# Moving the adaLN row sums into the retention loop, in batches of four

## The reference

```python
def reference(x, c, ..., w_ada, b_ada, final_g):
    c_act = jax.nn.silu(c)
    for l in range(DEPTH):
        mod = c_act @ w_ada[l] + b_ada[l]                   # 1024 -> 6 * 1024, one row
        shift1, scale1, gate1, shift2, scale2, gate2 = jnp.split(mod, N_MOD, axis=-1)
        h = _modulate(_rmsnorm(x, norm_mix_g[l]), shift1, scale1)
        x = x + gate1[:, None, :] * _mixer(h, w_in[l], w_ret_out[l], w_sb_out[l], w_mix_out[l])
        h2 = _modulate(_rmsnorm(x, norm_mlp_g[l]), shift2, scale2)
        u = jnp.square(jax.nn.relu(h2 @ w_up[l]))
        x = x + gate2[:, None, :] * (u @ w_down[l])
    return _rmsnorm(x, final_g)
```

## Time and profile before

| | us |
|---|---|
| median of 3 runs | 2580.16 (2579.53 to 2580.59) |
| the profiled execution, first to last instruction | 2577.3 |
| PE busy | 2436.3 (95%) |
| DVE busy | 1147.3 (45%) |
| ACT busy | 890.2 (35%) |
| POOL busy | 901.7 (35%) |

### The profile page before, as it was taken

One profiled execution on the slowest core, in us unless ns is written; L12 is line 12 of the kernel. 1 busy time (PEld: TensorE's weight loads), 2 busy tenths in 40 slices (PEclk: granted clock), 3 DMA queues, 4 the chain that ended last, 5 costly groups with the idle time before them and its releaser, 6 DMA issues.

```text
span 2577.3 us, 32158 instructions
## 1 busy us (share of the span) xinstructions
PE 2436.3 (95%) x11946; PEld 1991.6 (77%) x11946; DVE 1147.3 (45%) x1535; ACT 890.2 (35%) x1005; POOL 901.7 (35%) x382
## 2 busy tenths in 40 slices
PE   6999999999998889999979999999999988999898
PEld 5887887888877667777867888888888866777786
DVE  6343243144446872552454323233444487552623
ACT  2222222255582232222322222224556613222232
POOL 1333433433332323433433343333332323433342
PEclk7999999999999999999999999999999998999999
DMA  6222222211125633433222232222112354433421
GB/s 216 92 86 82 96 77 82 95 63 59 62 67 174 200 99 102 144 128 98 98 79 79 73 103 66 90 94 67 64 65 66 98 178 145 145 121 113 130 93 55
DMA packets 252462, 260.62 MB, mean 101 GB/s; under 512 B 4145, under 2 KB 250049, under 8 KB 252353
## 3 DMA queue, kind: packets, MB, share of 16 engines
q1 hardware_dynamic: 250816, 255.92, 30.7%
q10 hardware_dynamic: 1536, 3.17, 0.4%
HBM read 256.97 MB, written 2.10 MB: 101 GB/s over the span
## 4 chain that ended last, share of the span: by engine, by line
PE 73%; DVE 15%; issue 4%; ACT 4%; DMA 3%; DVEq 0%; SPq 0%; ACTq 0%
PE proj L695 45%; PE proj L732 11%; DVE ada_sum L962 8%; PE proj L717 5%; PE att L830 3%; PE att L784 3%; DVE work L1222 3%; PE att L815 2%; PE att L842 1%; PE att L771 1%; DMA w_raw<-in_w_mix_out 1%; DMA work<-in_w_ada 1%; DVE ada_sum L960 1%; ACT w_hi L403 1%; ACT y_hi L606 1%
## 5 line engine op out<-in xcount | busy, mean ns | idle before, releaser
L365 POOL TENSOR_TENSOR w_lo<-w_raw,w_hi 128x1024 fp32r<-128x1024 f32 x368 | 899.5, 2448 | 1637.4 <-ACT w_hi L403 1637.1
L695 PE MATMUL proj<-h_hi,w_hi 128*128 128x512 f32 x1472 | 591.7, 402 | 10.5 <-DVE x_T L1035 9.4
L403 ACT ACTIVATE w_hi<-w_raw 128x1024 fp32r<-128x1024 f32 x368 | 385.3, 1054 | 612.0 <-PE proj L695 443.7
L695 PE MATMUL proj<-h_hi,w_lo 128*128 128x512 f32 x1472 | 578.0, 393 | 0.0
L695 PE MATMUL proj<-h_lo,w_hi 128*128 128x512 f32 x1472 | 577.5, 392 | 0.0
L695 PE MATMUL proj<-y_hi,w_hi 128*128 128x512 f32 x832 | 333.1, 400 | 21.2 <-DVE y_lo L1225 21.0
L695 PEld LDWEIGHTS proj<-h_hi,w_hi 128*128 128x128 f32 x1472 | 279.3, 190 | 72.8 <-issue 13.5
L695 PE MATMUL proj<-y_lo,w_hi 128*128 128x512 f32 x832 | 329.7, 396 | 0.0
L695 PE MATMUL proj<-y_hi,w_lo 128*128 128x512 f32 x832 | 329.5, 396 | 0.0
L695 PEld LDWEIGHTS proj<-h_hi,w_lo 128*128 128x128 f32 x1472 | 278.9, 189 | 59.9
L695 PEld LDWEIGHTS proj<-h_lo,w_hi 128*128 128x128 f32 x1472 | 279.4, 190 | 59.2 <-issue 3.8
(11 more groups left out here) (147 smaller groups left out, 2630.3 us busy)
## 6 DMA issues: line engine op xcount, KB each, us to landing
w_raw<-in_w_in SPq DMA_DIRECT2D x88, 1024.0 KB, 5.1
work<-in_w_ada SPq DMA_DIRECT2D x56, 1024.0 KB, 5.3
w_raw<-in_w_up SPq DMA_DIRECT2D x32, 1024.0 KB, 6.1
w_raw<-in_w_down SPq DMA_DIRECT2D x32, 1024.0 KB, 5.0
w_raw<-in_w_ret_out SPq DMA_DIRECT2D x16, 1024.0 KB, 4.9
w_raw<-in_w_sb_out SPq DMA_DIRECT2D x8, 1024.0 KB, 6.3
w_raw<-in_w_mix_out SPq DMA_DIRECT2D x8, 1024.0 KB, 7.8
ya<-in_x SPq DMA_DIRECT2D x1, 2048.0 KB, 8.3
```

The lines of the kernel that those rows point to most:

```text
L365: pool.tensor_tensor(w_lo[:, s, :, :], w_raw[:, s // 2, :, P * (s % 2):P * (s % 2 + 1)], w_hi[:, s, :, :], ALU.subtract).then_inc(lo_ready, 1)
L403: act.activation(w_hi[:, 2 * s + j, :, :], w_raw[:, s, :, P * j:P * (j + 1)], ACT.Copy).then_inc(hi_ready, 1)
L695: last = pe.matmul(proj[:, j, :], w[:, slot, k, :], a[:, k, :], start=k == 0 and n == 0, stop=k == KT - 1 and n == 2)
```

## The change

All sums after the first 8 are made inside the retention loop, 12 per pass: four before each head's decay multiply, and four after the first four halves of the `w_ret_out` units. PE turns four sums at a time into bank 5 of `att` (8 matmuls), and DVE takes the eight columns with one addition. `ada_raw` and four slots of `ada_sum` now lie in a slab shared with `sp_hi` and `sp_lo`, which the retention loop doesn't use. The output, mix and MLP stages have no sums, turns, takes or loads of `w_ada`. PE waits for the new `ada_taken` before the third token block's product, since that writes bank 5. The number of sums and of turning matmuls is as before.

```diff
+ADA_BATCH = 4
+ADA_LOOP = 3 * ADA_BATCH
+ADA_CREDIT = 2
+ADA_STEPS = ADA_UNITS + ADA_CREDIT
...
-        sp_hi = sb("sp_hi", [P, 2, CAUSAL], f32r)
-        sp_lo = sb("sp_lo", [P, 2, CAUSAL], f32r)
+        slab = sb("slab", [P, 4 * CAUSAL])
+        sp_hi = nc.alloc_sbuf_tensor_at("sp_hi", [P, 2, CAUSAL], f32r, offset=slab_base)
+        sp_lo = nc.alloc_sbuf_tensor_at("sp_lo", [P, 2, CAUSAL], f32r, offset=slab_base + 8 * CAUSAL)
...
-        ada_raw = part(5120, 2, KT, UNIT)
+        ada_raw = slab[:, 0:2 * KT * UNIT].rearrange("p (s k n) -> p s k n", s=2, k=KT)
...
# SP
+            def load_ada(layer, i, k):
...
+                sp.wait_ge(ada_summed, ADA_STEPS * layer + ADA_LOOP * i + k - 1 + ADA_CREDIT)
+                sp.dma_start(ada_raw[:, k % 2:k % 2 + 1, :, :], src).then_inc(ada_in[k % 2], 16)
...
                             load(pair, 6 * j + n, w_in_cols(col))
+                            for k in ([], [], [], [0, 1], [2], [3])[n]:
+                                load_ada(layer, i, ADA_BATCH * j + k)
                     for m in range(4):
                         load(pair, 12 + m, wret_v[:, l1, ds(KT * i, KT), m * UNIT:(m + 1) * UNIT])
+                        for k in ([], [8, 9], [10], [11])[m]:
+                            load_ada(layer, i, k)
# PE
+            def turn_ada(layer, i, batch):
+                pe.wait_ge(ada_summed, ADA_STEPS * layer + ADA_LOOP * i + ADA_BATCH * (batch + 1) + ADA_CREDIT)
+                for q in range(ADA_BATCH):
                     for j in range(2):
+                        at = 2 * q + j
+                        last = pe.matmul(att[:, ADA_BANK, at:at + 1], ada_sum[:, q, j * P:(j + 1) * P],
                                          one_c[:, :], start=True, stop=True)
...
                         half_unit(pair, u + 4, 0, h_hi, h_lo)
+                        turn_ada(layer, i, h)
                         pe.wait_ge(probs_ready, head + 1)
...
                             if t == 2:
                                 half_unit(pair, u + 4, 1, h_hi, h_lo)
+                                pe.wait_ge(ada_taken, 6 * layer + 3 * i + h + 1)
...
                     for m in range(1, 4):
                         whole_unit(pair, 12 + m, y_hi, y_lo)
+                        if m == 2:
+                            turn_ada(layer, i, 2)
# DVE, retention loop
+                        for q in range(ADA_BATCH):
+                            sum_ada(layer, i, ADA_BATCH * h + q)
                         dve.wait_ge(decay_in, 16 * head + 16)
...
                         silu(0)
+                        take_ada(layer, i, h)
                         moments_of(0)
...
                             free(dve.tensor_tensor(ya[:, k, :], ya[:, k, :], proj[:, half, :], ALU.add), half)
+                            if k < ADA_BATCH:
+                                sum_ada(layer, i, 2 * ADA_BATCH + k)
+                    take_ada(layer, i, 2)
# DVE, output, mix and MLP stages
-                        due_ada()
-                        n = ada_of(m, half)
-                        if n is not None:
-                            sum_ada(layer, n, n % 2, n // 2)
```

More of the change, by code:

```diff
@@ L308, in _, with load_quarter @@
                     load(first, SB_OUT + m, (wsb_v if m < 4 else wmix_v)[:, l1, :, m % 4 * UNIT:(m % 4 + 1) * UNIT])
[L309 to L315, removed]
+                def load_quarter(pair, f):
                     for m in range(4):
                         load(pair, MLP + m, wup_v[:, l1, :, ds(f * D + m * UNIT, UNIT)])
[L318 to L324, removed]
                     for m in range(4):
@@ L883, in _, with quarter @@
                         half_unit(first, unit, half, hi, lo, tile_ready if half == 0 else None)
-                        turn_ada()
-                        n = ada_of(m, half)
-                        if n is not None:
-                            ada_pending[-1] = (layer, n, n % 2)
                 mean_square(2 * layer + 1, at_mlp)
-                def quarter(pair, f, with_ada):
+                def quarter(pair, f):
                     for m in range(4):
@@ L904, in quarter @@
                                       if m == half == 0 else None)
-                            turn_ada()
                 with pe.Fori(0, QUARTERS - 1) as f:
-                    quarter(first + 4 * f, f, True)
-                quarter(first + 4 * (QUARTERS - 1), QUARTERS - 1, False)
+                    quarter(first + 4 * f, f)
+                quarter(first + 4 * (QUARTERS - 1), QUARTERS - 1)
             mean_square(2 * DEPTH, at_layer)
@@ L1036, in add_to_x @@
                                               x_T[:, k, :], ALU.mult, ALU.add), half)
-            with own.loop(DEPTH, 326) as layer:
+            with own.loop(DEPTH, 302) as layer:
                 first = layer * LAYER_PAIRS
+                dve.sem_inc(ada_summed, ADA_CREDIT)
                 dve.wait_ge(x_turned, KT)
@@ L1043, in _ @@
                 norm(2 * layer, at_layer)
-                with own.loop(RET_LOOPS, 42) as i:
+                with own.loop(RET_LOOPS, 42 + 7 * ADA_LOOP) as i:
                     pair = first + RET_PAIRS * i
@@ L1184, in _ @@
                 gates = MODS * KT * layer
-                pending = []
-                def due_ada():
-                    pending.append(None)
-                    if len(pending) > 2 and (due := pending.pop(0)):
-                        take_ada(*due)
                 for m in range(8):
@@ L1207, in _ @@
                             add_to_x(first, SB_OUT + m, half, k, gates + KT * GATE1)
-                        due_ada()
-                        n = ada_of(m, half)
-                        if n is not None:
-                            sum_ada(layer, n, n % 2, n // 2)
-                            pending[-1] = (layer, n, n % 2)
                 scale_and_shift(layer, 1)
@@ L1226, in quarter @@
                                               ALU.subtract).then_inc(u_split, 1)
-                            due_ada()
-                            if half == 0 and not last:
-                                n = 4 * f + 12 + m
-                                sum_ada(layer, n, m % 2, 2 * f + 6 + m // 2)
-                                pending[-1] = (layer, n, m % 2)
                     for m in range(4):
@@ L1237, in quarter @@
                             add_to_x(pair, MLP + 4 + m, half, k, gates + KT * GATE2)
-                            due_ada()
-                with own.loop(QUARTERS - 1, 32) as f:
+                with own.loop(QUARTERS - 1, 0) as f:
                     quarter(first + 4 * f, f, False)
```

56 lines of the change are left out of this document (23 added, 33 removed).

## The result

The kernel before has a median of 2579.99 us (2579.53 to 2580.59, 4 runs), the changed one 2512.74 us (2511.92 to 2513.46, 4 runs). The ratio is 0.9737, with a 95% interval of 0.9723 to 0.9751. So 67 us are saved where 103 were forecast: the direction was right, the size was not, and 2512.7 lies above the range of 2456 to 2510. The profiled span fell from 2577.3 to 2510.0; the forecast for it was 2473.7.

A forecast was written before the change was run, and what follows sets the result against it. PE, busy 95% of the span, was taken as the bound, slowed by waits for DVE's sums. 136.4 - 17.8 - 8 - 3 - 4 = 103.6 saved gave a span of 2473.7 and a forecast of 2477 us, range 2456 to 2510.

The forecast's parts named there:

- The gain outside retention: Output, mix and MLP quarters of both layers, freed of sums, run at PE's own pace: 136.4 us saved.
- Output and mix: The output and mix stage without sums falls from 119.0 to 88.0 us, a gain of 31.0.
- The heads' sums: Four sums before each of eight heads' decay multiply fit DVE's idle time: cost 0, upper bound 24 us.
- The turns: 12 PE turns of four sums replace 48 of one, at 0.37 us each, hidden by nothing: 17.8 us saved outside retention.
- The rope table: Start of each layer's retention: two `w_ada` loads ahead delay the table, 2.0 us a layer, 4 us lost.
- The `w_ret_out` sums: Four sums in each of four `w_ret_out` passes make PE wait 2.0 us a pass: 8 lost, bounds 0 and 24.
- The term of 3 for the clock: `w_ret_out` passes: waits of 1 to 2 us bring some matmuls at 1.2 GHz, 0.7 us a pass, 3 lost.
- Two signs: Profile signs of a wrong prediction, among them sums of 8 us and more, and a rope wait growing over 3 us.
- Rival (a): Cover in the heads runs out, 24 us, and `w_ret_out` passes reach their bound, 16 more: 2517 us, chance 0.15.

The follow-up runs named there:

- e6: The changed kernel without the four adaLN sums of each second head (loads, semaphores and turns stay): 2512.1 us.
- e3: The changed kernel with the first two `w_ada` loads of each head issued behind the fifth unit's weight load: 2501.8 us.
- e1: The changed kernel with the last `w_ret_out` unit's weight load issued before the third `w_ada` load, not behind it: 2489.0 us.
- e7: The changed kernel with GpSimd's weight split cut to one of eight row blocks, the other low parts set to zero once: 2460.0 us.
- e8: The changed kernel with both load reorderings of e1 and e3, `w_ret_out` sums behind halves 1, 3, 4, 5 and the turn behind the last unit: 2467.3 us.

## Why the prediction was wrong

**The gain outside retention** held and was a little better: the spans differ by 67.3 and retention by 73.7 the other way, so 141.0 came from elsewhere, where 136.4 was the term (+4.6). Output and mix gained 31.9, against 31.0.

**The heads' sums** at 0 held: e6 shows it, and so does the first head, where the decay multiply started at 114.5, 5 us later than before and 2 later than forecast, and TensorE never waited for it. The law that was used, a sum of some 6 us with one GpSimd operation, was right too.

**The turns** were a term that was mis-sized: 1.5 us for a batch of four, from 0.37 for one. The second pass of heads, which has neither rope nor `w_ret_out`, grew by 3.9 us in layer 0 and 3.6 in layer 1 for two turns, so one in a head costs 1.9 and the eight 14.9 (twice 3.90 + 3.57), where 11.8 stood. The 0.37 of the earlier trace rows was the distance from the turn to the next product, and left out that the product behind that starts late too. Before, the row behind the last of the earlier trace rows (TensorE's timeline):

```profile
833.29 0.39 PE L695 MATMUL proj<-y_lo,w_hi 128*128 128x512 f32 x1
```

From the product at 832.98 to this one it is 0.31 in place of 0.23, so a turn of one sum moves the work by 833.29 - 832.61 - 0.23 = 0.45 us, and four by 1.8. That fits the 1.9.

**The rope table** was mis-sized: 4 was taken, with 0 and 5.4 a layer as bounds, and it cost 4.4 and 4.8, together 9.2 (the first pass of heads grew by 8.3 and 8.4, of which 3.9 and 3.6 are its two turns). The half megabyte was taken to suffer little "because the table comes by another queue". It was issued at 66.26, as early as before, but 3 us behind two loads of 1 MB each, and came 3.3 us later; e3, which moves just those loads, brings it back. The wait that grew also brought seven or eight products at 1.2 GHz, which the term left out. By the rule that was weighed (the Trainium skill, "DMA: Bandwidth & Descriptors", section "Issuing engines are not separate DMA queues") a separate queue is no separate engine, and this trace agrees with that: 3.3 us of delay. It doesn't agree with my reading of "interleave" as "little delay".

**The `w_ret_out` sums are the step that failed.** With their turn and the clock, 16.9 us were put for four stages, and they cost 73.7 - 9.2 - 14.9 = 49.6. That is 32.7 of the 36.3 us by which the span missed. The prediction had seen the late weight load ("issued 241, landing by 249, needed at 262") and that GpSimd's next operations come later by it, and held that harmless, since TensorE needs the unit late. It was issued at 249.4, in a stage that begins 8.3 us later than before, so it was nearly on time as forecast, and so was the first loss, 1.26 us behind sum 1 where 1.4 stood. What was left out is how GpSimd's delayed operations then lie: four close together, three of them on sum 4. "Meets POOL twice and ends at 258.0, 0.6 after PE asks for it" became three meetings, a start delayed 1.68 us by data, and a wait of 4.92 with the turn at half clock behind it. Had the load been held against the sums in place of TensorE's need, the clump could have been found: e1 shows that the order of two loads is 23.7 us, and e7 that GpSimd's share is the whole.

The sum of the misses, 32.7 + 5.2 + 3.1 - 4.6 = 36.4, is but for rounding the 36.3 us between the forecast span and 2510.0. The term of 3 for the clock was too low for the same reason: of the 11.7 us of a stage, 5.7 are more idling and the rest is the turn and what ran at 1.2 GHz. Two signs that the prediction named for being wrong came true: sums of 8 us and more (9.72), and a rope wait that grows by more than 3 us (3.3). Rival (a) gave about the measured time, 2517, but for another reason: its 24 us in the heads weren't there, and its bound of 6 us a stage for the sums was too small (10.5). The bound was made of additions that wait for a sum with one GpSimd operation beside it, and so it couldn't hold a sum with three.

By the Trainium skill ("SBUF — State Buffer", section "Who interferes with whom") a VectorE instruction with two inputs in SBUF contends with a GpSimd instruction that reads SBUF, for ports that are an exclusive lock, and one with at most one SBUF input doesn't. The traces agree: steps of 0.50 us that take 2.5 us, one for each GpSimd operation that holds one up, and additions with one input in PSUM (L1110) at 0.68 to 0.69 us, also beside GpSimd.

## What to carry to other kernels

Work moved onto an engine that shares something with a helper engine must be laid against that helper's timeline, operation by operation, and the helper's timeline is set by loads that the change itself may shift. A load that lands in time for its reader can still be too late or too bunched for others: ask of each load when its helpers will run and what runs beside them. An engine is late for all that stands behind a stretched instruction. So don't queue a small result between two urgent ones that follow each other closely, and leave a free slot behind it where there is one: e8 has no sum between the first unit's two additions, and a free half behind its first sum.

## What the runs showed of the hardware

- A VectorE sum of seven steps costs 3.61 us alone and about 2.02 us more for each GpSimd split of 2.40 us that holds up a step: 5.63, 7.65 and 9.72 with one, two and three. A split that begins as the sum's last step ends holds up none: the first head's fourth sum meets two and takes 5.64. GpSimd loses much less: two splits take 4.80 to 5.05 us beside a sum and 4.72 to 4.76 without one.
- TensorE's clock can fall behind one-column matmuls though the engine is busy without a hole. Behind the 16 records of a turn the six products that follow take 2.26 us in all eight heads; behind 32 records they take 3.64 to 4.48 in seven heads (3.68 at a granted clock of 0.60 in the first), and 2.26 still in one.
- The turn after an idle wait of 4.9 us runs at 1.2 GHz: 3.57 us in place of 1.84. Here a late result is paid three times, in idling, in its own reader and in the products that follow.
- Two loads of 1 MB on one queue delay a load of 512 KB on another that is issued about 3 us later by 3.3 us.
